# Weight buffers placed 0, 4, 8 and 12 bytes off, and matmul columns read and written in another order

## What is computed

```python
def swiglu_ffn(h, w_in, w_out):
    gate, up = jnp.split(jnp.einsum('bsd,df->bsf', h, w_in), 2, axis=-1)
    return jnp.einsum('bsf,fd->bsd', jax.nn.silu(gate) * up, w_out)

def second_block(x, ...):
    h = x
    for layer in range(DEPTH_2):
        hn = rmsnorm(h, norm_gains[layer, 0])
        mixed = fox_attention(...) if layer % N_MIXERS == 0 else hgrn2_recurrence(...)
        h = h + rmsnorm(mixed, norm_gains[layer, 1])
        hn = rmsnorm(h, norm_gains[layer, 2])
        h = h + rmsnorm(swiglu_ffn(hn, ffn_w_in[layer], ffn_w_out[layer]), norm_gains[layer, 3])
    return h
```

## Time and profile before

| | us |
|---|---|
| median of the runs (2) | 2200.8 |
| the profiled execution, its own time | 2200.2 |
| its span, first to last instruction | 2198.1 |
| TensorE matmul busy | 2138.4 (97%), 9588 matmuls |
| TensorE weight load busy | 1709.5 (78%), 9588 loads |
| GpSimd busy | 1498.2 (68%) |
| VectorE busy | 1117.0 (51%) |
| ScalarE busy | 663.2 (30%) |

### The profile page before, as it was taken

One profiled execution on the slowest core, in us unless ns is written; L12 is line 12 of the kernel. 1 busy time (PEld: TensorE's weight loads), 2 busy tenths in 40 slices (PEclk: granted clock), 3 DMA queues, 4 the chain that ended last, 5 costly groups with the idle time before them and its releaser, 6 DMA issues.

```text
span 2198.1 us, 26833 instructions
## 1 busy us (share of the span) xinstructions
PE 2138.4 (97%) x9588; PEld 1709.5 (78%) x9588; DVE 1117.0 (51%) x1982; ACT 663.2 (30%) x1142; POOL 1498.2 (68%) x741
## 2 busy tenths in 40 slices
PE   7999999999999999999999999999999999999997
PEld 3878777768888887788868888886788777888886
DVE  6899974884444103777643222105877835222101
ACT  3413335123222103444442111104555534111100
POOL 5868575667777887644379777886333348877785
PEclk9999999999999999999999999999999999999999
DMA  6323223732333332222123333332222222333332
GB/s 247 107 84 96 77 78 106 268 142 96 95 95 96 105 105 86 80 84 78 48 76 106 96 97 99 102 106 83 59 67 68 68 68 77 96 96 98 102 105 86
DMA packets 56371, 215.98 MB, mean 98 GB/s; under 512 B 6216, under 2 KB 6216, under 8 KB 53088
## 3 DMA queue, kind: packets, MB, share of 16 engines
q1 hardware_dynamic: 52992, 206.96, 29.3%
q10 hardware_dynamic: 3296, 7.91, 1.1%
HBM read 212.70 MB, written 2.15 MB: 98 GB/s over the span
## 4 chain that ended last, share of the span: by engine, by line
PE 78%; DVE 10%; POOL 4%; ACT 3%; issue 3%; DMA 2%; SPq 0%; DVEq 0%; POOLq 0%; ACTq 0%
PE ps L371 63%; DVE y L2036 3%; PE ps L603 2%; PE ps L1192 2%; DMA raw<-in_wstream 2%; PE ps L408 2%; POOL w_hi L974 1%; POOL w_lo L980 1%; PE ps L1284 1%; PE ps L1130 1%; PE ps L1315 1%; PE ps L1421 1%; PE ps L1302 1%; ACT u_hi L476 1%; DVE u_lo L526 1%
## 5 line engine op out<-in xcount | busy, mean ns | idle before, releaser
L980 POOL TENSOR_TENSOR w_lo<-raw,w_hi 128x1024 fp32r<-128x1024 f32 x335 | 813.6, 2429 | 199.3 <-ACT w_hi L1879 175.5
L974 POOL TENSOR_TENSOR w_hi<-raw,ones 128x1024 fp32r<-128x1024 f32 x304 | 582.9, 1918 | 368.9 <-DMA raw<-in_wstream 368.3
L371 PE MATMUL ps<-u_hi,w_hi 128*128 128x512 f32 x1760 | 708.9, 403 | 7.1 <-DVE qk L2047 2.8
L371 PE MATMUL ps<-u_hi,w_lo 128*128 128x512 f32 x1760 | 687.9, 391 | 0.0
L371 PE MATMUL ps<-u_lo,w_hi 128*128 128x512 f32 x1760 | 686.5, 390 | 0.0
L371 PEld LDWEIGHTS ps<-u_hi,w_hi 128*128 128x128 f32 x1760 | 332.1, 189 | 77.2 <-issue 6.7
L371 PEld LDWEIGHTS ps<-u_hi,w_lo 128*128 128x128 f32 x1760 | 331.1, 188 | 71.2
L371 PEld LDWEIGHTS ps<-u_lo,w_hi 128*128 128x128 f32 x1760 | 331.9, 189 | 66.9 <-issue 3.6
L371 PE MATMUL ps<-f_hi,w_lo 128*128 128x512 f32 x528 | 205.4, 389 | 0.0
L371 PE MATMUL ps<-f_hi,w_hi 128*128 128x512 f32 x528 | 205.4, 389 | 0.0
L371 PE MATMUL ps<-f_lo,w_hi 128*128 128x512 f32 x528 | 205.4, 389 | 0.0
(11 more groups left out here) (366 smaller groups left out, 2901.4 us busy)
## 6 DMA issues: line engine op xcount, KB each, us to landing
raw<-in_wstream SPq DMA_DIRECT2D x342, 512.0 KB, 3.6
ada_buf<-in_ada SPq DMA_DIRECT2D x16, 1024.0 KB, 7.3
ada_start<-in_ada SPq DMA_DIRECT2D x8, 1024.0 KB, 17.0
cbc<-decay_rows ACTq DMA_DIRECT2D x7, 512.0 KB, 3.5
x<-in_xT SPq DMA_DIRECT2D x1, 2048.0 KB, 8.0
bc<-gate_rows ACTq DMA_DIRECT2D x4, 512.0 KB, 5.3
out_T<-x ACTq DMA_DIRECT2D x8, 256.0 KB, 2.2
prm<-in_params SPq DMA_DIRECT2D x1, 357.5 KB, 2.9
```

What stands on the lines that cost most here:

```text
L371: last = nc.tensor.matmul(out, a, b, start=(start and k == 0 and i == 0), stop=(stop and k == nk - 1 and i == 2))
L974: g.tensor_tensor(w_hi[slot][:], raw[slot][:], ones[:, 0:1].to_broadcast([P, D]), ALU.mult).then_inc(chunk_hi, 1)
L980: g.tensor_tensor(w_lo[slot][:], raw[slot][:], w_hi[slot][:].bitcast(f32), ALU.subtract).then_inc(chunk_split, 1)
```

## The change

Two things are changed. First, each weight slot i starts 4 x i bytes behind a multiple of 32 bytes, for raw, w_lo and w_hi alike: slot 0 not at all, slot 1 by 4 bytes, slot 2 by 8, slot 3 by 12. For this the slots stand 4608 bytes apart, and small constants (mod, late_b, col_a, ident_b) fill two of the gaps; dg, fv and low_rows move into the area of m. Second, in the feed forwards of the second block the matmuls take their 512 columns in another order, the same for the moving operand and for the PSUM tile, so that every result stands where it stood. `backward` runs from the last column to the first. `two_up` takes columns 0 to 3, then 256 to 259, then 4 to 7, then 260 to 263, and so on. `two_down` takes 252 to 255, then 508 to 511, then 248 to 251, and so on. The feed forward of the attention layer (the second of the program) has `backward` in its up stage and `two_up` in its down stage; that of the recurrence layer (the third) has `two_down` up and `backward` down. The three chunks of each up stage in `gemm_first` keep the forward order, and the first feed forward keeps it throughout.

```diff
-    raw = [place(f"raw{i}", D) for i in range(SLOTS)]
-    w_lo = [nc.alloc_sbuf_tensor_at(f"w_lo{i}", [P, D], f32r, offset=here[0] - (SLOTS - i) * 4 * D) for i in range(SLOTS)]
-    w_hi = [place(f"w_hi{i}", D, f32r) for i in range(SLOTS)]
+    WIDE = D + 8
+    raw, w_lo, w_hi = [], [], []
+    slots_at = here[0]
+    for i in range(SLOTS):
+        here[0] = slots_at + i * (4 * D + 512)
+        raw.append(nc.alloc_sbuf_tensor_at(f"raw{i}", [P, WIDE], f32, offset=here[0])[:, i:i + D])
+        w_lo.append(nc.alloc_sbuf_tensor_at(f"w_lo{i}", [P, WIDE], f32r, offset=here[0])[:, i:i + D])
+        here[0] += 4 * WIDE
+        if i == 0:
+            mod, late_b = place("mod", 48), place("late_b", P, bf16)
+        elif i == 1:
+            col_a, ident_b = place("col_a", 6 * KT), place("ident_b", P, bf16)
+    slots_at += SLOTS * (4 * D + 512)
+    for i in range(SLOTS):
+        here[0] = slots_at + i * (4 * D + 512)
+        w_hi.append(place(f"w_hi{i}", WIDE, f32r)[:, i:i + D])
...
+    def backward(t, at_):
+        return bass.AP(t, at_ + T - 1, [[t.shape[1] * (t.shape[2] if len(t.shape) > 2 else 1), P], [-1, T]])
+
+    def two_down(t, at_):
+
+        return bass.AP(t, at_ + T // 2 - 4, [[t.shape[1] * (t.shape[2] if len(t.shape) > 2 else 1), P], [-4, T // 8], [T // 2, 2], [1, 4]])
+
+    def two_up(t, at_):
+        return bass.AP(t, at_, [[t.shape[1] * (t.shape[2] if len(t.shape) > 2 else 1), P], [4, T // 8], [T // 2, 2], [1, 4]])
...
-                gemm_chunk(pe, base + 4 * it + c, (base + c) % SLOTS, ps[c][:], u_tiles, u_lows, 0, KT, True, True, hook=hook)
+                if order is None:
+                    at_ = ps[c][:], u_tiles, u_lows
+                else:
+                    at_ = order(ps[c], 0), lambda k: order(u_hi, k * T), lambda k: order(u_lo, k * T)
+                gemm_chunk(pe, base + 4 * it + c, (base + c) % SLOTS, *at_, 0, KT, True, True, hook=hook)
...
-        ffn_pe(norms[3], C_UP2, C_DOWN2, {"g": (a_ff[0], "silu"), "a": (v_ff[0], "f")}, outs[3], (v_ff[0], "lo"))
+        ffn_pe(norms[3], C_UP2, C_DOWN2, {"g": (a_ff[0], "silu"), "a": (v_ff[0], "f")}, outs[3], (v_ff[0], "lo"),
+               backward, two_up)
...
-        ffn_pe(norms[5], C_UP3, C_DOWN3, {"g": (a_ff[1], "silu"), "a": (v_ff[1], "f")}, outs[5], (v_ff[1], "lo"))
+        ffn_pe(norms[5], C_UP3, C_DOWN3, {"g": (a_ff[1], "silu"), "a": (v_ff[1], "f")}, outs[5], (v_ff[1], "lo"),
+               two_down, backward)
```

More of the change, by code:

```diff
@@ L136, in build @@
     prm = place("prm", NPRM)
-    mod = place("mod", 48)
     cvec = place("cvec", KT)
-    col_a = place("col_a", 6 * KT)
     zero_col = place("zero_col", KT)
@@ L144, in build @@
     ident = place("ident", P)
-    ident_b = place("ident_b", P, bf16)
-    late_b = place("late_b", P, bf16)
     early = place("early", P)
@@ L152, in build @@
     x = place("x", KT * T, shape=[KT, T])
-    raw = [place(f"raw{i}", D) for i in range(SLOTS)]
-    w_lo = [nc.alloc_sbuf_tensor_at(f"w_lo{i}", [P, D], f32r, offset=here[0] - (SLOTS - i) * 4 * D) for i in range(SLOTS)]
-    w_hi = [place(f"w_hi{i}", D, f32r) for i in range(SLOTS)]
+    WIDE = D + 8
[14 more added lines that the diff above has]
+        w_hi.append(place(f"w_hi{i}", WIDE, f32r)[:, i:i + D])
+    here[0] = slots_at + SLOTS * (4 * D + 512)
     u_hi = place("u_hi", KT * T, f32r, [KT, T])
@@ L184, in build @@
     bc = place("bc", 2 * T, shape=[2, T])
-    dg = place("dg", T, shape=[NT, P])
     WOFF = [0, 512, 896, 1152]
@@ L197, in build @@
     cA, cB = [place(n, T) for n in ("cA", "cB")]
+    dg = place("dg", T, shape=[NT, P])
     assert here[0] <= mix_end
@@ L220, in build @@
     q_hi, q_lo = [[(t[b], qz[2 * j + b]) for b in range(2)] for j, t in enumerate((q_hi, q_lo))]
-    fv = place("fv", T)
     va_both = place("va_both", 8 * P, f32r, [2, NT, P])
-    low_rows, weighed = place("low_rows", T), place("weighed", T)
+    weighed = place("weighed", T)
     pt_hi = [place(f"pt_hi{i}", NT * T, f32r, [NT, T]) for i in range(2)]
@@ L231, in build @@
     pr = [place(f"pr{i}", T) for i in range(2)]
+    fv, low_rows = place("fv", T), place("low_rows", T)
     assert here[0] <= mix_end
@@ L564, in norm_dve, with out_pe @@
             low(KT - 1)
-    def out_pe(pe, og, base, ks, hi, lo, ready=None, extra=None):
+    def out_pe(pe, og, base, ks, hi, lo, ready=None, extra=None, order=None):
         nch = len(ks)
@@ L575, in out_pe @@
                     c = s * nch + j
-                    gemm_chunk(pe, base + og_body * nch * it + c, (base + c) % SLOTS, ps[s % 2][:],
+                    gemm_chunk(pe, base + og_body * nch * it + c, (base + c) % SLOTS, order(ps[s % 2], 0) if order else ps[s % 2][:],
                                lambda k, o=sum(ks[:j]): hi(o + k), lambda k, o=sum(ks[:j]): lo(o + k), 0, nk,
@@ L1217, in _, with ffn_pe @@
                 ada_pe(pe, turn)
-        def ffn_pe(N, base, dbase, read, og, prev):
+        def ffn_pe(N, base, dbase, read, og, prev, order=None, down=None):
             def read_wait(j, name, s):
@@ L1243, in ffn_pe @@
             pe.wait_ge(S.sem, S.at("f", FT - 2))
-            out_pe(pe, og, dbase, DOWN_K, lambda k: f_hi[:, k, :], lambda k: f_lo[:, k, :],
-                   ready=lambda k: pe.wait_ge(S.sem, S.at(step, k)))
+            if down is None:
+                at_ = lambda k: f_hi[:, k, :], lambda k: f_lo[:, k, :]
+            else:
+                at_ = lambda k: down(f_hi, k * T), lambda k: down(f_lo, k * T)
+            out_pe(pe, og, dbase, DOWN_K, *at_, ready=lambda k: pe.wait_ge(S.sem, S.at(step, k)), order=down)
         norm_pe(pe, norms[1], outs[0], lambda: ada_pe(pe, 3))
```

## The result

The changed kernel takes 2253.2 us, the median of 2 runs (2252.9 and 2253.5), against 2200.8 us. The ratio is 1.0238 with a 95% interval from 1.0194 to 1.0282: it got slower, though the interval leaves open whether by more than 2%, and the time lies 8 us beyond the range that was given. The span is 2250.8 us against 2198.1.

The account below looks back on a forecast made before the run. TensorE's back-to-back matmuls, 226.7 ns from start to start, were taken to bound the kernel. Every term was put at 0, so 2200.2 us plus 0, with the median 0.6 us above, gave 2201 us; range 2118 to 2245 us.

Parts of the forecast that it names:

- What bounds the kernel: TensorE, busy throughout all six feed forward windows at 2.4 GHz; the path is the distance between matmul starts, 226.7 ns.
- The count: Feed forwards 2 and 3: 984 reordered matmuls per up stage, 528 per down stage, 3024 in all, 3.0 us per ns.
- Column order: Feed forwards 2 and 3: 1512 matmuls backward and 1512 by pieces of four would keep their pace, 0 us.
- the row with the two-piece operand: Profile row of a moving operand in two pieces of 64 columns: four matmuls last 0.61 us, against 0.60 with one piece.
- upper bound of 3 ns per break: Pieces of four: each of the 127 breaks in a matmul's column order costs at most 3 ns.
- the point of decision for half the matmuls: Rival 1 decides from 44 us, which is 29 ns on each matmul of one half of the 3024.
- Four bytes off, TensorE: 6032 weight loads starting 4, 8 or 12 bytes later cost 0; bounds -10 ns and +3 ns.
- GpSimd and DMA off their place: GpSimd's chunk work stays at 1.90 + 2.40 us, and a longer DMA landing than 3.6 us would be covered: 0.
- Rival 1: Feed forwards 2 and 3: backward or broken order loses one column per cycle; 2508 us, or 2815 us; chance 0.17.
- the small losses: 3 ns per weight load off its place (2219 us) or 10 ns per broken order (2216 us); chance 0.03.
- Rival 2: Weight load and moving operand collide; offsets part them, 2141 or 2118 us, chance 0.17; order alone, 2171 us, chance 0.05.
- its sign: Rival 2 would show in the first feed forward too, with a matmul distance that goes in turns of four chunks.

Follow-up runs that it names:

- e2_orders: The changed kernel with its column orders kept and all weight slots put back on a multiple of 32 bytes: 2245.4 us against 2198.5 before the change.
- e1_offsets: The changed kernel without its orders: weight slots 0, 4, 8 and 12 bytes off, all columns forward; 2219.5 us against 2198.5 before the change.
- e7_narrow_loads: Kernel before, but feed forwards 2 and 3 load only 96, 64, 32 and 32 columns of each weight tile in their four stages: 2213.5 us.
- e11_more_places: Kernel before, all columns forward, but weight slots 0 to 3 stand 16, 48, 128 and 80 bytes off: 2225.1 us.

## Why the prediction was wrong

**What bounds the kernel** was right, and so was the measure. TensorE at full clock, without a pause, one matmul each 226.7 ns: what was lost is just the number of matmuls times the change of that distance.

**The count** was right: 984 and 528 matmuls per stage, 3.0 us per ns on 3024.

**Column order, sized 0, measured 47 us** (e2_orders). This is the term that failed, in both its parts. "A run of adjacent columns stays a run of adjacent columns" was not evidence on backward: it costs 6.7 ns, 10 us for the 1512. For pieces of four the row with the two-piece operand was read as a price of about nothing per break. It is a plain float32 matmul, at half the pace, and it has a single break; it says nothing on 127 breaks in a stream that comes at twice the pace. The prediction had itself set out that the split stream is the only one at that pace. The upper bound of 3 ns per break held (23 to 27 ns against 381), and so did the point of decision for half the matmuls, 29 ns: the pieces of four came to 36 us (down 2 and up 3 of the changed kernel), and backward and the offsets carried the sum over 44.

**Four bytes off, TensorE, sized 0, measured 21 us alone** (e1_offsets). The argument was that many addresses give one pace. All of these were multiples of 512 bytes apart, which the prediction said, and then leaned on all the same. The loss lay just in the bits that had never been varied: 3.3 to 5.4 ns per matmul on a slot that is off in up stage 1, and up to 6.6 in the down stages, against a stated bound of 3.

**GpSimd and DMA off their place, sized 0**: right, 1.89 and 2.36 to 2.39 us, 3.6 us to landing.

**Rival 1** had the right sign and the right mechanism, a stream that loses its pace, at the wrong price. It took the plain pace of 430 ns as the only alternative, so it gave 2508 us. Because that price was so far off, nothing stood between 2245 us and 2508, and the small losses, which are what happened, had a chance of 0.03. The range ended at the edge of 2% and not at a bound of the costs: with its own bound of 3 ns on 6032 loads and, say, 10 ns on each of 3024 orders it would have reached 2249 us, and a break priced between its two bounds would have reached further.

**Rival 2**, that the 13.3 ns are two streams meeting and can be won back: nothing was won back by less load (e7_narrow_loads) or by any place or order tried. That the two streams meet is not excluded by this. Its observation, that the distance isn't rigid, was right, and its sign came too, a distance that goes in turns of four chunks in the first feed forward, but upward; the mean of a stage only ever rose. Here the trace also limits the Trainium skill (TensorE: Matmul & The Clock Gate, Part 2), by which the weight load has its own read port and takes no read bandwidth from the running matmul: moving only the weights changed the matmul's distance by up to 6.7 ns, though a shorter load gave nothing back. By which path they disturb each other no run shows.

What stays open is where the 13.3 ns above 213.3 come from in the best case, which rule sets the price of a place, and what gives one and the same place two paces. A moving operand off its place with high and low part off alike, a weight load with the columns reversed, or matmuls in a row on one load weren't tried. No version faster than the kernel before was found.

## What to carry to other kernels

When a kernel is nothing but one instruction back to back, a few per cent per instruction are the whole result, so an unmeasured access pattern on it must not be put at zero: the range should run from nothing to the nearest measured loss. Keep operands of float32r matmuls on the same large alignment (here the same place in every 512 bytes) and read them straight upward; if an order must be changed, change it on the PSUM side, which was free, or in runs of 64 columns, which kept 226.7 ns. That many addresses gave one pace says nothing about address bits that were the same in all of them.

## What was not expected of the hardware

- A moving operand read backward costs 6.7 ns per 512 columns (233.3 against 226.7), and the same backward order in PSUM costs nothing.
- Pieces of 2 columns, read and written, bring a matmul of 512 columns to 339.8 ns, pieces of 64 leave it at 226.7.
- A weight load of 32 columns instead of 128 makes the matmul beside it slower, 231.6 against 226.7 ns.
- Losses of place and order do not add: 21 and 47 us alone, 52 together.
- The same slot against the same moving operand has two paces, 227.1 and 233 ns (e11_more_places), most likely by what went before it.
- A weight load of 309 ns, longer than the distance of the matmuls, raises that distance by only 8.3 ns, to 235.0.
